# Adding the causal mask on VectorE, and interleaving the first and last steps of three attentions with dense units

## What is computed

```python
# fox: 16 heads of 64, a learned bias cum[q] - cum[k] on the scores
s = einsum('bhqd,bhkd->bhqk', q_blk, k) * scale + cum_blk[..., None] - cum[:, :, None, :]
p = softmax(where(key_pos <= qpos, s, -inf));  o = p @ v
# diff: 8 heads, two score maps each
p = softmax(where(causal, s, -inf));  a = p[:, :, 0] - lam * p[:, :, 1];  o = a @ v
# nsa: 16 heads, each with a "selected" and a "window" attention. With 512 tokens
# both reduce to plain causal attention; the outputs are gated and added
p = masked_softmax(s, mask);  o = gate * (p @ v)
```

## Time and profile before

| | |
|---|---|
| median of 3 runs | 2538.97 us (2534.74 to 2539.65) |
| profiled execution, its own time | 2536.68 us |
| its span (first to last instruction) | 2534.9 us |
| what lies around the span | 1.78 us |
| TensorE (PE) busy | 2472.0 us |
| VectorE (DVE) busy | 1412.4 us |
| ScalarE (ACT) busy | 972.3 us |
| mean granted TensorE clock | 0.996 of 2.4 GHz |
| chain that ended last, share of PE | 83% |

### The profile page before, as it was taken

The page is one execution under the profiler, slowest core; times in us unless marked ns, Lnnn a source line. Parts: engine busy times, 40 slices in busy tenths (PEclk is TensorE's granted clock), DMA queues, the critical chain, the costliest instruction groups (busy, mean ns, idle before and its releaser), DMA issues.

```text
span 2534.9 us, 33524 instructions
## 1 busy us (share of the span) xinstructions
PE 2472.0 (98%) x12104; PEld 1964.4 (77%) x12104; DVE 1412.4 (56%) x2035; ACT 972.3 (38%) x1704; POOL 187.4 (7%) x316
## 2 busy tenths in 40 slices
PE   9999999999999999999999999999998999999999
PEld 7877777888887876788888787778886658888887
DVE  5655436777426345677752788646555654442432
ACT  4333423333323345344331335534345652431331
POOL 0000000000000013000000200300001540000000
PEclk9999999999999999999999999999999999999999
DMA  4322232333332320333333232032222002232332
GB/s 132 83 67 75 83 95 83 97 99 99 108 99 70 96 75 1 93 98 98 92 116 100 80 97 78 27 123 75 78 81 59 1 1 90 85 99 93 98 99 101
DMA packets 278502, 210.91 MB, mean 83 GB/s; under 512 B 12228, under 2 KB 234097, under 8 KB 278385
## 3 DMA queue, kind: packets, MB, share of 16 engines
q1 hardware_dynamic: 270465, 198.64, 26.7%
q10 hardware_dynamic: 7920, 10.70, 1.3%
...
## 4 chain that ended last, share of the span: by engine, by line
PE 83%; issue 7%; DVE 5%; ACT 3%; DVEq 1%; POOL 1%; POOLq 1%; DMA 0%; ACTq 0%
PE PS L161 14%; PE PS L163 14%; PE PS L162 14%; PE PS L158 9%; PE PS L159 9%; PE PS L160 9%; PE PS L1484 2%; PE PS L1513 2%; PE PS L1504 2%; ACT WH L149 1%; POOLq L2139 1%; DVE WL L154 1%; PE PS L2227 1%; PE PS L1473 1%; PE PS L555 0%
## 5 line engine op out<-in xcount | busy, mean ns | idle before, releaser
L154 DVE TENSOR_TENSOR WL<-RAW,WH 128x1024 fp32r<-128x1024 f32 x352 | 431.3, 1225 | 730.4 <-ACT WH L149 724.0
L149 ACT ACTIVATE WH<-RAW 128x1024 fp32r<-128x1024 f32 x362 | 383.2, 1058 | 1027.6 <-PE PS L160 578.1
L161 PE MATMUL PS<-XH,WH 128*128 128x512 f32 x1568 | 618.9, 395 | 3.4 <-DVE XL L663 1.4
L163 PE MATMUL PS<-XH,WL 128*128 128x512 f32 x1568 | 612.0, 390 | 0.0
L162 PE MATMUL PS<-XL,WH 128*128 128x512 f32 x1568 | 611.9, 390 | 0.0
L161 PEld LDWEIGHTS PS<-XH,WH 128*128 128x128 f32 x1568 | 295.5, 188 | 69.5 <-issue 4.9
L163 PEld LDWEIGHTS PS<-XH,WL 128*128 128x128 f32 x1568 | 295.2, 188 | 62.3
L162 PEld LDWEIGHTS PS<-XL,WH 128*128 128x128 f32 x1568 | 295.4, 188 | 60.2 <-issue 1.0
L158 PE MATMUL PS<-WH,XH 128*128 128x512 f32 x416 | 165.9, 399 | 4.8 <-DVE CPOS L2655 2.7
L159 PE MATMUL PS<-WH,XL 128*128 128x512 f32 x416 | 163.2, 392 | 0.0
L160 PE MATMUL PS<-WL,XH 128*128 128x512 f32 x416 | 163.1, 392 | 0.0
...
## 6 DMA issues: line engine op xcount, KB each, us to landing
...
```

The lines of the kernel that those rows point to most:

```text
L149: act.activation(WH[:, slot, :], RAW[:, slot, :], ACT.Copy).then_inc(hi_ready, 1)
L154: dve.tensor_tensor(WL[:, slot, :], RAW[:, slot, :], WH[:, slot, :], ALU.subtract).then_inc(lo_ready, 1)
L161: pe.matmul(o, wh, ah, start=first, stop=False)
L163: return pe.matmul(o, wl, ah, start=False, stop=last)
```

## The change

1. The mask matmuls with `MROW` are gone. A new tile `ROWMASK` (128x512: zeros, and the causal triangle in the last 128 columns) is made by GpSimd twice, once for fox and diff and once for NSA. `pair_masked_dve` takes the place of `pair_maxima_dve`: for each head and query block one `tensor_tensor_reduce` reads scores and mask, writes their negated sum to P in SBUF and gives the negated row maximum. `pair_exps_act` then reads and writes P in place with scale -1.
2. TensorE's next scores wait for `mx` in place of `ex`.
3. Four subs (turn 0 and sub 0 of turn 1) in place of three, one or two are computed among the last dense units ahead of each attention: in fox before units 6 and 7 of `foxv`; in diff before and in the middle of unit 23; in NSA before units 42 and 43. VectorE takes two of the four evacuations behind the last unit, and ScalarE the other two.
4. While the last two turns drain, TensorE computes the first dense unit of the next stage in two halves: `rows_first_pe` after fox, unit 0 of `mix2` after diff, two of eight steps of `merge` after NSA.
5. In diff, VectorE's order is changed: weights 2 and two of the three combinations move to the next turn, and weights 0 now stands ahead of the masked sub 1.
6. The last two sigmoid gates ahead of NSA move behind it, so that exp's table is loaded earlier.

```diff
+
+    def row_mask_pool(pool, k):
+
+        pool.memset(ROWMASK[:, :], 0.0)
+        pool.drain().then_inc(row_mask.zero, 1)
+        pool.wait_ge(row_mask.zero, k + 1)
+        pool.affine_select(out=ROWMASK[:, SEQ - P:SEQ], in_=ROWMASK[:, SEQ - P:SEQ], compare_op=ALU.is_ge,
+                           fill=MASKED, base=0, pattern=[[-1, P]], channel_multiplier=1)
+        pool.drain().then_inc(row_mask.ready, 1)
+
     def pair_scores_pe(pe, s, t, sub, query, key, bias=None):
         if 3 * t + sub >= 2:
-            pe.wait_ge(s.ex, s.at.ex + 3 * t + sub - 1)
-        for hh in range(2):
-            for k, (qb, c0) in enumerate(SUBS[sub]):
-                pe.matmul(pair_score(t, sub, hh, c0 + qb * P, P), IDB[:, :], MROW[:, :],
-                          start=k == 0, stop=False, skip_group_check=True)
-        for qb, c0 in SUBS[sub]:
+            pe.wait_ge(s.mx, s.at.mx + 3 * t + sub - 1)
+        for k, (qb, c0) in enumerate(SUBS[sub]):
             n = (qb + 1) * P
             if bias is not None:
                 for hh in range(2):
-                    pe.matmul(pair_score(t, sub, hh, c0, n), *bias(t, hh, n), start=False, stop=False,
+                    pe.matmul(pair_score(t, sub, hh, c0, n), *bias(t, hh, n), start=k == 0, stop=False,
                               skip_group_check=True)
-        for qb, c0 in SUBS[sub]:
+        for k, (qb, c0) in enumerate(SUBS[sub]):
             n = (qb + 1) * P
             for hh in range(2):
-                last = pe.matmul(pair_score(t, sub, hh, c0, n), query(t, hh, qb), key(t, hh, n), start=False,
-                                 stop=True, skip_group_check=True)
+                last = pe.matmul(pair_score(t, sub, hh, c0, n), query(t, hh, qb), key(t, hh, n),
+                                 start=bias is None and k == 0, stop=True, skip_group_check=True)
         last.then_inc(s.sc, 1)
...
         act.wait_ge(s.mx, s.at.mx + i + 1)
-        if sub == 0 and t >= 2:
-            act.wait_ge(s.tr, s.at.tr + chunks * (t - 1))
         for qb, c0 in SUBS[sub]:
             n = (qb + 1) * P
             for hh in range(2):
                 col = 8 * (t % 2) + NMCOL[qb] + hh
-                last = act.activation(Px[:, t % 2, hh, POFF[qb]:POFF[qb] + n], pair_score(t, sub, hh, c0, n),
-                                      ACT.Exp, bias=NM[:, col:col + 1], accum_out=RS[:, col:col + 1])
+                p = Px[:, t % 2, hh, POFF[qb]:POFF[qb] + n]
+                last = act.activation(p, p, ACT.Exp, scale=-1.0, bias=NM[:, col:col + 1], accum_out=RS[:, col:col + 1])
         last.then_inc(s.ex, 1)
...
+            if t < n and 3 * t + 2 >= begun:
                 pair_exps_act(act, s, t, 2, Px)
             if 1 <= t <= n:
                 act.activation(*pair_copy(act, s, t - 1, 4, PTx), ACT.Copy).then_inc(s.pa, 1)
-    def pair_maxima_dve(dve, s, t, sub):
+    def pair_masked_dve(dve, s, t, sub, Px, M, chunks=5):
+
         i = 3 * t + sub
         dve.wait_ge(s.sc, s.at.sc + i + 1)
+        if sub == 0 and t >= 2:
+            dve.wait_ge(s.tr, s.at.tr + chunks * (t - 1))
         for qb, c0 in SUBS[sub]:
             n = (qb + 1) * P
-            col = 8 * (t % 2) + NMCOL[qb]
-            last = dve.tensor_reduce(NM[:, col:col + 2], PS[:, 2 * (i % 2):2 * (i % 2) + 2, c0:c0 + n], AX, ALU.max, negate=True)
+            for hh in range(2):
+                col = 8 * (t % 2) + NMCOL[qb] + hh
+                last = dve.tensor_tensor_reduce(out=Px[:, t % 2, hh, POFF[qb]:POFF[qb] + n],
+                                                in0=pair_score(t, sub, hh, c0, n), in1=M[:, SEQ - n:SEQ], scale=-1.0,
+                                                scalar=3e38, op0=ALU.add, op1=ALU.min, accum_out=NM[:, col:col + 1])
         last.then_inc(s.mx, 1)
...
             if n == 5:
+                dve.wait_ge(row_mask.ready, 1)
                 for sub in range(2):
-                    pair_maxima_dve(dve, fa, 0, sub)
+                    pair_masked_dve(dve, fa, 0, sub, PB, ROWMASK)
                 for sub in range(2):
                     pair_weights_dve(dve, fa, 0, sub)
             elif n == 6:
-                pair_maxima_dve(dve, fa, 0, 2)
+                pair_masked_dve(dve, fa, 0, 2, PB, ROWMASK)
+                pair_masked_dve(dve, fa, 1, 0, PB, ROWMASK)
                 pair_weights_dve(dve, fa, 0, 2)
+                pair_weights_dve(dve, fa, 1, 0)
+        dve.wait_ge(unit_done, first["foxv"] + 8)
+        for c in range(2, NC_):
+            dve.tensor_copy(VT[:, c, 512:1024], PS[:, 4 + c, :]).then_inc(fv.left, 1)
...
+    def fox_out_pe(pe, k):
+        if k == 0:
+            pe.wait_ge(fa.mx, fa.at.mx + 3 * KT)
+        rows_first_pe(pe, "foxout", OH, OL, 0, k)
     def fox_act(act):
...
-            unit_tm(pe, bd, 0, 0, n, lambda c: PS[:, 4 * (body % 2) + c, :], 2 * u, before, tiles_pe(pe, n3, X) if body == 0 else None)
+                pe.wait_ge(rd.ev, rd.at.ev + 12)
+                diff_scores_pe(pe, 0, 1)
+
+            def amid(k):
+                if k == KT - 1:
+                    diff_scores_pe(pe, 0, 2)
+                    diff_scores_pe(pe, 1, 0)
+            unit_tm(pe, bd, 0, 0, n, lambda c: PS[:, 4 * (body % 2) + c, :], 2 * u, before,
+                    tiles_pe(pe, n3, X) if body == 0 else amid if n == 23 else None)
             if n in (13, 17, 21):
...
-                pair_maxima_dve(dve, da, 0, 0)
             if n in DROPES:
                 drope_dve(dve, DROPES[n])
+            if n == 21:
+                drope_dve(dve, 14)
+            elif n == 22:
+                pair_masked_dve(dve, da, 0, 0, PBD, ROWMASK, 3)
+                pair_masked_dve(dve, da, 0, 1, PBD, ROWMASK, 3)
+                pair_weights_dve(dve, da, 0, 0)
+                drope_dve(dve, 15)
+                pair_weights_dve(dve, da, 0, 1)
+            elif n == 23:
+                pair_masked_dve(dve, da, 0, 2, PBD, ROWMASK, 3)
+                pair_masked_dve(dve, da, 1, 0, PBD, ROWMASK, 3)
+                diff_combine_dve(dve, 0, 0)
+                dve.wait_ge(unit_done, bd + n + 1)
+                for c in range(2, NC_):
+                    dve.tensor_scalar(DV[:, c, 512:1024], PS[:, 4 + c, :], BY_ROOT[:, c:c + 1], None,
+                                      ALU.mult).then_inc(ld.left, 1)
...
     def diff_dve(dve):
-        for t in range(KT + 1):
-            if 1 <= t < KT:
-                pair_maxima_dve(dve, da, t, 0)
-            if t:
-                diff_combine_dve(dve, t - 1, 2)
+        for t in range(1, KT + 1):
+            if 1 < t < KT:
+                pair_masked_dve(dve, da, t, 0, PBD, ROWMASK, 3)
+            pair_weights_dve(dve, da, t - 1, 2)
+            diff_combine_dve(dve, t - 1, 1)
+            diff_combine_dve(dve, t - 1, 2)
             if t < KT:
-                pair_maxima_dve(dve, da, t, 1)
                 pair_weights_dve(dve, da, t, 0)
-            if t:
-                dve.tensor_copy(*diff_copy(dve, t - 1, 0)).then_inc(da.pd, 1)
+                pair_masked_dve(dve, da, t, 1, PBD, ROWMASK, 3)
+            if t == 2:
+                lo(dve, bd, 0, 0, 23)
+            dve.tensor_copy(*diff_copy(dve, t - 1, 0)).then_inc(da.pd, 1)
             if t < KT:
-                if t == 0:
-                    lo(dve, bd, 0, 0, 23)
+                diff_combine_dve(dve, t, 0)
+                pair_masked_dve(dve, da, t, 2, PBD, ROWMASK, 3)
                 pair_weights_dve(dve, da, t, 1)
-                pair_maxima_dve(dve, da, t, 2)
-                diff_combine_dve(dve, t, 0)
-                diff_combine_dve(dve, t, 1)
-                pair_weights_dve(dve, da, t, 2)
...
-            if n == STEPS2 - 1:
-                pe.wait_ge(sgn, 6)
+            if n == STEPS2 - 2:
+                pe.wait_ge(r0.tmp, r0.at.tmp + KT + 6)
                 pe.wait_ge(rk.ev, rk.at.ev + 2 * NSA_G)
-                for sub in range(2):
-                    pair_scores_pe(pe, na, 0, sub, nsa_query, nsa_key)
+            if n >= STEPS2 - 2:
+                for i in range(2 * (n - STEPS2 + 2), 2 * (n - STEPS2 + 2) + 2):
+                    pair_scores_pe(pe, na, i // 3, i % 3, nsa_query, nsa_key)
             unit_fm(pe, b2, 0, 0, n, PS[:, gate2_bank(m), :], XH, XL)
...
-                for sub in range(2):
-                    pair_maxima_dve(dve, na, 0, sub)
+            if n == STEPS2 - 3:
+                dve.wait_ge(row_mask.ready, 2)
+            if STEPS2 - 3 <= n < STEPS2 - 1:
+                begun = [divmod(i, 3) for i in range(2 * (n - STEPS2 + 3), 2 * (n - STEPS2 + 3) + 2)]
+                for t, sub in begun:
+                    pair_masked_dve(dve, na, t, sub, PN, ROWMASK)
+                for t, sub in begun:
+                    pair_weights_dve(dve, na, t, sub)
             jj = (n - GA) // 2 - 1
...
-        pair_pe(pe, na, 2 * NPAIR, PN, PTN, nsa_query, nsa_key, value, None, compressed, 2, begun=2)
+        def begin_merge(pe, k):
+            if k == 0:
+                pe.wait_ge(na.mx, na.at.mx + 6 * NPAIR)
```

(3 more changed lines are left out.)

241 lines of the change are left out of this document (141 added, 100 removed).

## The result

The changed kernel takes 2512.46 us in the median (2512.25 to 2513.18, 4 runs) against 2537.78 us of the kernel before beside it (2534.74 to 2539.65, 4 runs): a ratio of 0.9902, with a 95% interval of 0.9885 to 0.9919. Run again later beside three experiments it gave 0.9911 (0.9895 to 0.9926). So it is some 23 to 25 us faster; 10 had been forecast. The time lies in the range, at its lower end, and nearer to rival B (2500) than to the forecast.

A forecast was written before the change was run, and what follows sets the result against it. TensorE was taken to bound fox and NSA, and diff nearly. Steady turns +5.5 us and seams −15.5 us summed to −10.0, taking 2538.97 to 2529.0 us; the range was 2510 to 2543.

The forecast's parts named there:

- rival B: Everywhere: TensorE stays the bound and diff's wait goes; 19.8 us in turns, 19 at the seams, 2500 us; chance 0.12.
- the seams: Starts and ends of fox, diff and NSA: interleaved work fills TensorE's waits, −15.5 us in sum.
- the turns: Steady turns grow to 9.09 us in fox, 8.79 in NSA, 7.96 in diff; together +5.5 us.
- f: Fixed cost of VectorE's masked operation with its accumulator read: 0.19 us, the middle of bounds 0.13 and 0.27.
- p: ScalarE's exps reading SBUF instead of PSUM: 0.05 us more each, 0 as the lower end.
- Diff's sum: Diff's turn: VectorE waits for exps 0 ahead of masked 1; 7.96 us against 7.55.
- The mask's price: TensorE's mask matmuls: 0.75 us a turn, 24 us in 32 turns; floors 7.97 in fox, 7.92 in NSA.
- rival C: Slower: same VectorE-ScalarE ring, dearer accumulator read; a loss from f = 0.24, 2545 us at 0.27; chance 0.18.
- NSA's start: TensorE's 4.85 us wait for exps is filled by two further subs' scores; gain 6.1 us.
- the three ends: Next stage's work under the last turns fills TensorE's waits: 1.6 us in fox, 3.8 in diff, 0.6 in NSA.
- diff's start: Two more subs done ahead of the attention; gain 2.5 us.
- D: No change: the seams don't pay, TensorE only moves its wait, +5.5 eats the rest; 2534 to 2544 us; chance 0.20.

The follow-up runs named there:

- the run with the reciprocals: The changed kernel with a one-column reciprocal on VectorE behind each masked operation, 256 in all; 2525.5 us, ratio 0.9949 to the kernel before.
- taking its link out: The changed kernel with copy 1 and masked sub 2 ahead of the reciprocals of sub 1 in fox and NSA; 2506.16 us, ratio 0.988.
- the combined run: The changed kernel with masked 2 earlier and the weight tile's step later in fox and NSA, and diff's combination 2 later from turn 3; 2507.43 us.
- the run without them: The changed kernel with the next stage's first dense unit (in NSA the merge steps) issued whole behind the last values; 2519.02 us, ratio 0.9931.
- two runs: The changed kernel with third and fourth subs' scores behind the last dense unit, 2521.55 us; with the next stage's first unit behind the last values, 2519.02 us.
- the halves: The change split in two, against the kernel before: the mask alone, 2530.89 us, and the seams alone, 2530.90 us.
- diff's order: The changed kernel with VectorE's order in diff from turn 1 on as in the kernel before; 2518.58 us, ratio 0.9921 to the kernel before.
- the mask alone: The kernel before with only the mask moved to VectorE, exps in place and TensorE waiting for mx; 2530.89 us, ratio 0.9976.
- the seams alone: The changed kernel with the mask back on TensorE and the old maxima and exps, interleaving and diff's new order kept; 2530.90 us, ratio 0.998.

## Why the prediction was right in sign and range, and short in size

The direction, and the range, were right. The size was short by 13 to 15 us. Two things in this are luck. The sign of the total was carried by the seams; for the turns the forecast had +5.5 us, a loss, and they gave a gain. And the range held because two errors went against each other. Put what was measured for f and p (0.08 and 0.04, below) into the prediction's own sums, with TensorE's floor where the chain lies under it, and they give −13 for the turns and −20 for the seams, about 2505 us, under the range's lower end: the seams gave less than their term.

**The step that failed** is "so I take the middle, f = 0.19", and with it the lower bound of 0.13. Measured, f is 0.08. The bound added the slot of a whole small operation for the read of the accumulator; the read starts together with the next operation and costs 0.01 to 0.02 us. It lies outside both of the prediction's bounds, 0.13 and 0.27. With f at 0.08 the prediction's own sums give 7.27 + 0.64 + 0.30 = 8.21 us for fox (measured 8.19) and 6.97 + 0.64 + 0.30 = 7.91 for NSA (7.93). At f = 0.15, in the run with the reciprocals, they give 8.77 and 8.47 (8.68 and 8.38). The term p was sized nearly right: two exps of 512 start 0.72 us apart after (972.13, 972.85) and 0.68 before (971.75, 972.43), so p is 0.04; with it the first two sums are 8.15 and 7.85. So the mechanism, the chain from VectorE over ScalarE and back, stands: it was shown by lengthening it and by taking its link out, which gave the 7.97 of TensorE's floor. Forecast for the steady turns was +5.5 us. They gave 5 x −0.53, 13 x −0.70 and 5 x −0.17, −12.6.

**Diff's sum** (6.80 + 4f + 8p = 7.96) was wrong in its mechanism too. It let VectorE wait 1.48 us for exps 0 in every turn; the combinations moved to that place cover the wait. The chain that bounds the stage goes over GpSimd instead, and gives 7.38. The feared wait is real, and came up in the combined run, where its cover was gone. With f = 0.08 and p = 0.04 the sum gives 7.44; that it comes near to 7.38 is chance.

**The mask's price**, 0.75 us a turn, held: fox's floor was measured at 7.97. TensorE's busy time fell by 22 us. The rest of the 0.75 comes once for each group of masks: in the kernel before, two mask matmuls start 0.056 us apart (968.883 and 968.939), and the next matmul starts 0.149 later, so that two take 0.21 and four 0.33, which is 0.056 for each and about 0.10 for the group. The Trainium skill's row ("VectorE: DVE Perf Modes", the table of the section on the TRN2 errata) gives an estimate of 0.056 us for each, 134 cycles at 2.4 GHz, and the trace agrees. The 14 us that the prediction made of it leave out the 0.10 for each group. The advice to minimise the count of operations ("Rules for kernel authors" of the same page of the Trainium skill), which spoke for rival C, weighs little here, since the accumulator's reads cost next to nothing: 16 instructions for 4 cost VectorE 14.4 us in the whole kernel, 0.45 a turn.

**The seams** were put at −15.5. By the stages they gave: NSA's start −5.7 to the first maxima of turn 2, the prediction's own mark (−6.1), the three ends 5.9 in the run without them (6.0), diff's start −0.1 to the scores of turn 4 (−2.5). Fox's start gave −1.7 to the scores of turn 2, the masks of two turns in it (−0.9), and all but 0.1 of that was gone one turn later, behind the weight tile. In diff TensorE waits for ScalarE's two evacuations of the values, which now stand behind the exps of two subs; nothing in the prediction had it. TensorE after:

```profile
1574.34 3.50 PE L1914 MATMUL PS<-IDF,TK 128*128 128x128 f32 x16 [2.70 <-ACT DV L1982]
```

Behind the wait the granted clock is 0.50, and the 16 transposes take 3.50 us where they took 1.97 before. In fox the stall of 2.2 us behind the weight tile lies in the turns and stood in no term. The two waits make near to 5 us, and the slower transposes 1.5 more.

**The rivals.** B asked for f of at most 0.09 in fox and 0.12 in NSA, and f is 0.08: NSA is 0.05 over TensorE's floor and nearly at B, fox 0.2 over it, and diff is not at B at all. B was given 0.12, since the lower bound was taken for firm. C turns at 0.24, far off. The claim behind D, that ends and starts don't pay, is refuted by two runs for the changed kernel; with the old mask they paid 4.6 us together, with diff's new order.

**That the halves don't add** (4.6 and 4.6, together 23 to 25) had not been considered. Of the difference diff's order explains 2.5 to 5 us, by experiment. NSA's start explains part (the changed kernel's −6.4 against +2.0 and −2.2): with the mask alone exps begin behind a table load, so TensorE's wait grew to 6.1; with the seams alone the clock was down. The clock is a large part of what is left. The ten executions with the mask alone had a mean granted clock of 0.991 (0.989 to 0.993), where the kernel before, the seams alone and the changed kernel have 0.995 or, with the seams alone, 0.996. Among the ten, each 0.001 less went with about 2.3 us more. Carried to 0.995, outside what they span, that puts the mask alone at about 2522 us, 13 under before, within the 12 to 16 expected of it, though its diff turns are longer than expected. This is an estimate from ten executions. Which waits bring the clock down there, and how much time that costs by itself, no run separates; between diff and NSA, where the edit changes nothing, it cost the profiled execution 3.2 us against before, and the other two 1.6. What the remainder consists of was not settled.
